# Reordered ends of the attention stages in a one-core float32 transformer kernel on Trainium2

## The reference

```python
def diff_attention_blocks(q, k_all, v_all, lam):          # first block, 8 heads
    s = jnp.einsum("bqhcd,bkhcd->bchqk", q_blk, k_all) * scale
    p = jax.nn.softmax(s, axis=-1)
    attn = p[:, 0] - lam * p[:, 1]
    return jnp.einsum("bhqk,bkhe->bqhe", attn, v_all)
...
y = rms_norm(o, subln, 1e-5) * (1.0 - lam_init)
x = x + gate * ((y.reshape(B, T, 1024) * jax.nn.silu(g)) @ w_out)
...
def hybrid_layer(x, mem, norm_g, w_in, w_out, mem_norm_g, w_mem_kv, qk_g):   # second block, 2 layers
    proj = rms_norm_2(x, norm_g) @ w_in          # q, k, v, gate of each attention
    ...                                          # moba (6 heads), dilated (6 heads)
    mkv = rms_norm_2(mem, mem_norm_g) @ w_mem_kv # memory of 256 tokens, 4 heads
    y = concat([oa * silu(a_g), ob * silu(b_g), om * silu(m_g)])
    return x + y @ w_out
```

## Time and profile before

| | |
|---|---|
| median of 3 runs | 2387.86 us (2383.27 to 2391.37) |
| the profiled execution | 2388.85 us, span of its trace 2387.0 us |
| busy: PE, DVE, ACT, POOL | 86%, 55%, 47%, 30% |
| mean granted TensorE clock | 0.962 of full |
| chain that ended last, by engine | PE 57%, DVE 19%, ACT 12%, issue 8%, POOL 3%, DMA 1% |
| head 7 of `Diff`, to the last k-slice of its output | 1578.4 to 1633.2 us |
| first output stage, to the next norm's end | 1633.2 to 1682.4 us |
| second block, layer 0 and layer 1 | 1682.4 to 2045 us and 2045 to 2387 us |

### The profile page before, as it was taken

One profiled execution on the slowest core, in us unless ns is written; L12 is line 12 of the kernel. 1 busy time (PEld: TensorE's weight loads), 2 busy tenths in 40 slices (PEclk: granted clock), 3 DMA queues, 4 the chain that ended last, 5 costly groups with the idle time before them and its releaser, 6 DMA issues.

```text
span 2387.0 us, 56898 instructions
## 1 busy us (share of the span) xinstructions
PE 2058.7 (86%) x24624; PEld 1583.7 (66%) x24624; DVE 1304.5 (55%) x2181; ACT 1118.4 (47%) x1861; POOL 708.8 (30%) x417
## 2 busy tenths in 40 slices
PE   6999998688878888878899999979899889899889
PEld 3877776567666677656676666647566666666666
DVE  3288787634334444443456667672566652466752
ACT  5476676433333343332354454553455453455552
POOL 2344544100022030233332222333433332443433
PEclk9999999899999999998999999989999989899999
DMA  7233646633332322223131111103222211222122
GB/s 298 89 121 122 185 131 186 184 99 91 113 102 72 83 67 74 60 96 124 60 105 55 54 45 58 54 23 115 75 67 79 65 61 71 71 80 71 62 71 71
DMA packets 162313, 221.35 MB, mean 93 GB/s; under 512 B 84592, under 2 KB 116336, under 8 KB 161296
## 3 DMA queue, kind: packets, MB, share of 16 engines
q1 hardware_dynamic: 151920, 177.99, 24.4%
q0 software_dynamic: 8992, 36.57, 5.1%
q10 hardware_dynamic: 1152, 3.15, 0.4%
HBM read 164.98 MB, written 42.21 MB: 87 GB/s over the span
## 4 chain that ended last, share of the span: by engine, by line
PE 57%; DVE 19%; ACT 12%; issue 8%; POOL 3%; DMA 1%; ACTq 0%; DVEq 0%; POOLq 0%; SPq 0%
PE ps L272 8%; PE ps L274 7%; PE ps L273 7%; PE ps L1605 3%; PE ps L1595 2%; PE ps L1627 2%; PE ps L421 2%; DVE Y L1768 2%; PE ps L2607 2%; PE ps L2545 1%; PE ps L3186 1%; ACT DE L1725 1%; ACT p L2627 1%; PE ps L3144 1%; DVE pc L3262 1%
## 5 line engine op out<-in xcount | busy, mean ns | idle before, releaser
L257 POOL TENSOR_TENSOR wbl<-wb,wbh 128x1024 fp32r<-128x1024 f32 x122 | 294.6, 2416 | 652.7 <-ACT wbh L251 652.7
L1768 DVE COPY_PREDICATED Y<-rc,ps 128x512 f32<-128x512 int32 x120 | 85.5, 732 | 196.3 <-ACT DE L1725 135.0
L272 PE MATMUL ps<-hT2h,wbh 128*128 128x512 f32 x416 | 180.5, 434 | 10.6 <-POOL wbl L257 10.6
L272 PE MATMUL ps<-hTh,wah 128*128 128x512 f32 (+1 forms) x512 | 179.5, 351 | 10.9 <-POOL wal L257 10.9
L273 PE MATMUL ps<-hTl,wah 128*128 128x512 f32 (+1 forms) x512 | 173.8, 340 | 0.0
L274 PE MATMUL ps<-hTh,wal 128*128 128x512 f32 (+1 forms) x512 | 173.6, 339 | 0.0
L274 PE MATMUL ps<-hT2h,wbl 128*128 128x512 f32 x416 | 164.6, 396 | 0.0
L273 PE MATMUL ps<-hT2l,wbh 128*128 128x512 f32 x416 | 164.0, 394 | 0.0
L1942 POOL TENSOR_TENSOR ro<-ro 128x768 f32<-128x768 f32 x6 | 10.9, 1813 | 496.8 <-DVE ro L365 496.8
L251 ACT ACTIVATE wbh<-wb 128x1024 fp32r<-128x1024 f32 x122 | 128.2, 1052 | 61.9 <-PE ps L2225 43.4
L257 POOL TENSOR_TENSOR wal<-wa,wah 128x1024 fp32r<-128x1024 f32 x34 | 104.0, 3059 | 175.8 <-ACT wah L251 175.8
(11 more groups left out here) (466 smaller groups left out, 5399.5 us busy)
## 6 DMA issues: line engine op xcount, KB each, us to landing
wb<-in_w_in SPq DMA_DIRECT2D x56, 512.0 KB, 3.5
wm<-in_ada SPq DMA_DIRECT2D x48, 512.0 KB, 5.7
s_str_dram<-s POOLq DMA_DIRECT2D x42, 576.0 KB, 8.7
bkv<-s_str_dram SPq DMA_DIRECT2D x96, 192.0 KB, 3.3
wa<-in_rw_in SPq DMA_DIRECT2D x34, 512.0 KB, 3.8
wb<-in_da_in SPq DMA_DIRECT2D x32, 512.0 KB, 3.5
ARI<-s_str_dram SPq DMA_DIRECT2D x96, 128.0 KB, 3.6
wb<-in_w_out SPq DMA_DIRECT2D x16, 512.0 KB, 3.5
```

Source lines behind the costliest of these rows:

```text
L257: e.tensor_tensor(lo, self.raw[:, n % 3], hi.bitcast(F32), ALU.subtract).then_inc(self.K.s.w_lo, 1)
L272: e.matmul(z, wh[:, k, :], hi[:, k, a:b], start=k == 0, stop=False)
L1768: e.copy_predicated(self.Y[:, l - 1], twice(self.mY[l - 1]), banks[:, :, 0:256]).then_inc(v, 1)
```

## The change

It is all in the order of instructions, in eight places.

1. `exp_ln` is called right behind each SiLU, in `Diff.act_project` and in `Second.act_project`, and no longer just ahead of the next exponential.
2. In head 7 ACT's copies of quarters 0 and 1 come ahead of the exponentials of quarters 2 and 3, and head 6's end moves back, with its sums in bank 2; ACT takes head 7's squares from PSUM.
3. The splits of the output's blocks 41 to 43 come two steps later.
4. `products_ahead` takes slices 0 to 5 of two blocks, then slice 6 of both, then the third block.
5. In pairs 7 and 15 PE draws four parts right behind the first scores; ACT's splits of the output's blocks stand behind the exponentials 3, 5 and 7.
6. In the output stages the splits of the next blocks start at k = 1 and end at k = 6, one per k.
7. There the memory's squares and sums are spread over k = 0 to 5, and its tail is done in two pieces, at k = 6 and 7, on ACT, DVE and POOL.
8. The second layer's memory has its own place in SBUF and is loaded before block 83, when pair 6 has its values.

```diff
 def products_ahead(K, e, W, n, x, banks, free, ready):
+    for j, k in [(j, k) for j in range(2) for k in range(6)] + [(0, 6), (1, 6)] + [(2, k) for k in range(7)]:
+        if k == 0:
+            e.wait_ge(K.s.w_lo, W.lo0 + n + j + 1)
...
         e.activation(self.gb[b][:, :], psum[:, (i + 8) % 3, :], ACT.Silu).then_inc(s.evac_a, 1)
+        K.exp_ln(e)
...
         for qt in range(4):
-            if qt < 2:
+            if qt < 2 and h < 7:
                 scores(qt + 2)
             yield
...
                          psum[:, 3, :].rearrange("p (n c) -> p n c", c=128), ACT.Copy).then_inc(s.tr_a, 1)
+            if qt < 2 and h == 7:
+                scores(qt + 2)
+                if qt == 0:
+                    self.act_end(e, 6)
...
         for _ in attend(7):
-            if 0 < h < 4:
-                ahead(40 + h)
+            if 2 < h < 6:
+                ahead(38 + h)
...
         e.activation(self.gb[b][:, :], psum[:, (i + 5) % 3, :], ACT.Silu).then_inc(s.evac_a, 1)
+        K.exp_ln(e)
...
-            if P % 8 == 7 and z:
-                run(some(ahead, 2))
+            if P % 8 == 7:
+                run(some(ahead, 2 if z else 4))
...
-        if P % 8 == 7:
-            self.W.split_hi(e, self.block(P) + 5)
...
-            if P % 8 == 7 and z in (1, 2):
-                if z == 2:
+            if P % 8 == 7 and z in (1, 3, 5):
+                if z == 5:
                     e.wait_ge(s.nr_mul, o["nr_mul"] + self.scaled(P + 1))
-                self.W.split_hi(e, self.block(P) + 5 + z)
+                self.W.split_hi(e, self.block(P) + 5 + z // 2)
...
     def act_out(self, e, l):
         for k in range(8):
-            if k >= 3:
-                self.W.split_hi(e, 81 + 40 * l + k)
             if l < 1:
+                e.wait_ge(s.evac_v, ev + k + 1)
+                nx.act_square(e, k)
...
+                for m in {0: (0, 1, 2), 3: (3, 4, 5), 4: (6, 7)}.get(k, ()):
+                    nm.act_square(e, m)
+                if k >= 6:
+                    run(some(tail, 5))
+            if 0 < k < 7:
+                self.W.split_hi(e, 83 + 40 * l + k)
...
     def dve_out(self, e, l):
-            if k >= 3:
-                run(some(tail, 2))
+            if k >= 6:
+                run(some(tail, 5))
...
     def pool_out(self, e, l):
+            if 0 < k < 7:
+                self.W.split_lo(e, 83 + 40 * l + k)
+            if k >= 6:
+                run(some(tail, 3))
...
-            if n == 83:
-                e.wait_ge(s.yt_lo, self.c0["yt_lo"] + 8)
+            if n == 82:
+                e.wait_ge(s.pv_mm, self.c0["pv_mm"] + 7)
                 e.dma_start(self.mem[1][:, :, :], K.T["mem"]).then_inc(s.mem_in, 16)
```

More of the change, by code:

```diff
@@ L293, in products_ahead @@
 def products_ahead(K, e, W, n, x, banks, free, ready):
-    for j, bank in enumerate(banks):
-        e.wait_ge(K.s.w_lo, W.lo0 + n + j + 1)
-        free(j)
-        for k in range(7):
-            ready(k)
-            product_part(K, e, W, n + j, x, k, bank)
-            yield
+    for j, k in [(j, k) for j in range(2) for k in range(6)] + [(0, 6), (1, 6)] + [(2, k) for k in range(7)]:
+        if k == 0:
+            e.wait_ge(K.s.w_lo, W.lo0 + n + j + 1)
+            free(j)
+        ready(k)
+        product_part(K, e, W, n + j, x, k, banks[j])
+        yield
 def turn_halves(e, out, x, sem):
@@ L2563, in turn @@
                 e.wait_ge(s.sm_df, 4 * z + 4)
-                if qt == 0 and h:
+                if qt == 0 and 0 < h < 7:
                     e.wait_ge(s.rb_m, self.rb.done(h - 1))
@@ L2576, in pe_attend @@
         yield
-        if h:
+        if 0 < h < 7:
             self.pe_end(e, h - 1)
@@ L2587, in pe_attend @@
                 fill(2)
+            if qt == 0 and h == 7:
+                self.pe_end(e, 6)
             yield
@@ L2613, in pe_end, with sums @@
         e.wait_ge(s.pv_sq, h + 1)
-        self.rb.pe(e, h, K.psum[:, 3, :], K.ones, self.sq[2][:, :])
+        self.rb.pe(e, h, self.sums(h), K.ones, self.sq[2][:, :])
+    def sums(self, h):
+        return self.K.psum[:, 2 if h == 6 else 3, :]
     def act_attend(self, e, h):
@@ L2646, in act_attend @@
         e.wait_ge(s.pv_mm, h + 1)
-        e.activation(self.x2[:, h, :], psum[:, 2 if h == 7 else 3, :], ACT.Copy).then_inc(s.pv_c, 1)
+        if h == 7:
+            e.wait_ge(s.pv_n, h)
+            e.activation(self.sq[2][:, :], psum[:, 2, :], ACT.Square).then_inc(s.pv_sq, 1)
+            e.activation(self.x2[:, h, :], psum[:, 2, :], ACT.Copy).then_inc(s.pv_c, 1)
+            yield
+            return
+        e.activation(self.x2[:, h, :], psum[:, 3, :], ACT.Copy).then_inc(s.pv_c, 1)
         e.wait_ge(s.pv_c, h + 1)
@@ L2654, in act_end @@
     def act_end(self, e, h):
-        self.rb.act(e, h, self.K.psum[:, 3, :], self.R[2][:, :], 1e-5, 128.0)
+        self.rb.act(e, h, self.sums(h), self.R[2][:, :], 1e-5, 128.0)
     def dve_attend(self, e, h):
@@ L2700, in dve_attend @@
                 turn(qt - 1)
-            if qt == 0 and h:
+            if qt == 0 and 0 < h < 7:
                 self.dve_end(e, h - 1)
+            if qt == 1 and h == 7:
+                self.dve_sums(e, 6)
             if qt < 2:
                 scores(qt + 2)
+            if qt == 1 and h == 7:
+                self.dve_end(e, 6)
             yield
@@ L2710, in dve_sums @@
     def dve_sums(self, e, h):
-        self.rb.dve_first(e, h, self.K.psum[:, 3, :], self.sq[2][:, :], self.R[2][:, :], 1e-5, 128.0)
+        self.rb.dve_first(e, h, self.sums(h), self.sq[2][:, :], self.R[2][:, :], 1e-5, 128.0)
     def dve_end(self, e, h):
@@ L2720, in pool_attend @@
     def pool_attend(self, e, h):
-        for _ in range(4):
-            yield
-        if h:
-            self.pool_end(e, h - 1)
-        for _ in range(7):
+        for z in range(11):
+            if h and z == (6 if h == 7 else 4):
+                self.pool_end(e, h - 1)
             yield
@@ L2836, in __init__ @@
         with ExitStack() as cl:
-            self.mem = [K.sb(cl, "mem0", [8, 256], at=diff.end), K.sb(cl, "mem1", [8, 256])]
+            self.mem = [K.sb(cl, "mem0", [8, 256], at=diff.end)]
             for l in range(2):
@@ L3321, in pe_out @@
                                lambda j: e.wait_ge(s.evac_v, ev + k - 2)))
-            if l < 1 and k < 3:
-                for m in range(3 * k, min(3 * k + 3, 8)):
-                    self.nm[l + 1].pe_sum(e, m)
             if l < 1 and k:
                 self.nx[l + 1].pe_sum(e, k - 1)
+            if l < 1:
+                for m in {2: (0, 1, 2), 4: (3, 4, 5), 5: (6, 7)}.get(k, ()):
+                    self.nm[l + 1].pe_sum(e, m)
         if l < 1:
@@ L3335, in act_out @@
         for k in range(8):
-            if k >= 3:
-                self.W.split_hi(e, 81 + 40 * l + k)
             if l < 1:
+                e.wait_ge(s.evac_v, ev + k + 1)
+                nx.act_square(e, k)
                 if k == 0:
                     e.wait_ge(s.mem_in, 16 * l + 32)
-                if k < 3:
-                    for m in range(3 * k, min(3 * k + 3, 8)):
-                        nm.act_square(e, m)
-                else:
-                    run(some(tail, 2))
-                e.wait_ge(s.evac_v, ev + k + 1)
-                nx.act_square(e, k)
+                for m in {0: (0, 1, 2), 3: (3, 4, 5), 4: (6, 7)}.get(k, ()):
[4 more added lines that the diff above has]
+                self.W.split_hi(e, 83 + 40 * l + k)
         if l < 1:
-            self.W.split_hi(e, 89 + 40 * l)
             run(nx.act_tail(e))
@@ L3375, in pool_out @@
         for k in range(8):
-            if k >= 3:
-                self.W.split_lo(e, 81 + 40 * l + k)
-            if k >= 3:
-                run(some(tail, 1))
+            if 0 < k < 7:
+                self.W.split_lo(e, 83 + 40 * l + k)
+            if k >= 6:
+                run(some(tail, 3))
         if l < 1:
-            self.W.split_lo(e, 89 + 40 * l)
             run(self.nx[l + 1].pool_tail(e))
```

4 lines of the change are left out of this document (added).

## The result

After the change the kernel takes 2430.89 us (median of 4 runs, 2425.31 to 2437.52); the kernel before took 2389.45 on the same chip. The ratio is 1.0179, with a 95% interval of 1.0146 to 1.0212: **41 us, 1.8% slower**. The forecast was 2414.5 with a range of 2397 to 2435, so the sign and the range held, and the size was too small by 16 us.

A forecast was written before the change was run, and what follows sets the result against it. Behind the first block's attention PE was taken to be on most of the chain. 15.6 + 1.0 - 7.5 - 5.0 + 0.4 + 11.2 = +15.7, +25.7 with the clock: 2388.85 + 25.7 = 2414.5 us, range 2397 to 2435.

The forecast's parts named there:

- The load behind the gate: Second block, table load between gate and copy: the copy PE waits for comes 1.42 later, +15.6 us in two layers.
- The drain's rival: Rival, chance 0.04: each load at 12 second-block places also costs a 1.38 drain, 16.6 us more, 2431 us.
- The clock: Second block: PE's longer wait at the values brings slow stretches at 4 of 14 places, 2.55 each, +10 us.
- Pairs 7 and 15: Last pair of each layer: new wait of 3.7 for block 81 against gains elsewhere, +0.5 each, +1.0 us together.
- Head 7: First block's head 7: exponentials no longer wait for the norm, PE's waits 3.6 instead of 11.1, -7.5 us.
- The output stages, end: Both output stages, k = 6: DVE's last add stands behind splits and memory rows, +5.6 each, 11.2 us together.
- The output stages, early part: Output stages before the fourth product: -5.0 us in layer 0, where memory lies ready; +0.4 in the first stage.
- Part covered: Rival, chance 0.08: work between pairs waits for something later anyway; 15.6 goes, no clock loss, 2389 us.
- other side: Rival, chance 0.06: the values' 1.42 and the last add's 5.4 are absorbed by later waits; only gains remain, 2377.7 us.

The follow-up runs named there:

- the good parts: Kernel before plus head 7's order, load behind Diff's gate, product parts' order, early memory load, and in Second the load behind the copy: 2372.10 us, ratio 0.9940.
- the run with the old pair: Kernel after with pairs 7 and 15 put back as in the kernel before, load behind the gate kept: 2419.62 us, ratio 1.0148.
- the old stage: Kernel after with the output stages put back as in the kernel before, the memory's early load kept: 2418.18 us, ratio 1.0148.

## Why the prediction was right, and where not

- **The load behind the gate.** Right in mechanism and nearly to the figure. PE's wait is 2.16, and apart from new falls of the clock the way to pair 6's values grows by 8.3 to 9.1 per layer, for 9.2; pairs 0 to 3 grow by 0.9 to 1.15 each, for 1.25 and 1.42. The drain's rival fell, though it is its 2431 that the time hit, by chance: the load takes 1.28, 0.01 behind the gate and 0.02 ahead of the copy, where the Trainium skill (ScalarE: Activation LUTs, What ACT_TABLE_LOAD costs) adds some 1380 ns to it. In the heads of `Diff` it cost nothing: 51.15 us from one SiLU's load to the next before (1418.80 to 1469.95), 51.12 after (1413.07 to 1464.19).
- **The clock.** Right in kind, too small: four falls were assumed, and there are 8 at the 14 places (6 to 8 in each of the seven other runs with the wait). In the two stretches to pair 6 and pair 14, 35.6 measured less 2 x 9.1 leaves 17 us (19 with the 8.3), where the forecast had 10 for all places. The single fall costs 1.6 to 1.7 in a pair, less than my 2.55, but falls come behind other waits too, above all from pair 5 to pair 6, where both layers together lose 10.5 (38.0 for 32.74). Summed over the second block, the clock that is missing is 27 us before, 50 after, 33 without the load and 20 in the good parts. This is an upper bound of what it costs, as PE is idle in some of them.
- **Pairs 7 and 15.** The step that failed. "PE gets there after 2.4 and waits 3.7" was right (3.66), and so were the late split and the start of the second scores (7.1 behind pair 6's values, 6.85 before). Without the clock that working gave +3.0, which is 1.6 in the stretch of the table, and 2.1 and 2.9 are measured. Wrong was to credit 3.2 for the slow stretch behind the wait of 4.28: in this stretch 3.4 us of clock are missing before and 3.4 after, in both layers, since new slow stretches stand behind the values and behind the wait for block 81. And "one part less ahead of the last values (0.7)" was counted as a gain, while the parts drawn early are missing at the end, where PE's wait for the last slice grows from 0.52 to 2.9 and the clock falls behind it. Set against the run with the old pair, in which the wait of 4.28 is 2.4, the pair and its stage cost 4.6 and 5.3 (90.6 - 86.0, 68.8 - 63.5), some 10 us in all.
- **Head 7.** The other step that failed, on the other side: "I put these at 3.6 in place of 2.70 + 8.38 = 11.1" gave -7.5, and it is -2.2. I had followed ACT alone. DVE's stream, with three operations slowed beside POOL ahead of the difference, holds the same wait of 8. It is not the whole of it: with the three moved away 4.8 of the wait go and 0.8 of the head. What sets its length then stays open.
- **The output stages, end.** Right: +5.6 each forecast, 5.9 measured at the wait, by the chain as written. Only the place was not the one named: "PE's 6.50 there becomes 12", while the 6.50 stays and a wait of 6.54 stands ahead of the last sum. The whole stage costs 7.4 and 7.0, of which 0.95 is that sum at the low clock. The runs add that this chain hides a second one: without it, 3.9 of the 5.9 in the two waits stays.
- **The output stages, early part.** -5.0 forecast for the memory, and its early load is worth 4.5 with the old stage. Beside it the new order of the sums costs 0.6 in the first stage (7.4 less 5.9 and 0.95), for "+0.4", and 0.1 in layer 0.
- **The other rivals.** Part covered and other side fell: the 1.42 arrives at pairs 0 to 3 but for 0.3 to 0.5, and the 6.50 did not shrink.

The misses of head 7 (5.3), of the last pairs (3.0 and 3.8), of the clock (7 and what follows) and of the stages (1.4, 1.9, 1.6) all go the same way and make some 24 us. The executions' -5.8 up to head 7 goes the other way; 44.2 between the two spans less the forecast's 25.7 is 18.5.

## What to carry to other kernels

An operation that is moved off a busy place is not free at its new one: look at who waits for the next instruction of that stream. The same table load cost 24 us between a gate and the copy that TensorE waited for, and nothing one instruction later, in idle time. When two waits trade places, compare chains and not waits: work that fills one wait can be missing in the next, and what is queued behind the new wait decides. And a wait whose releaser is fixed may just get another, so read the streams of all engines that take part in it.
